# The prompt's memory projection laid into the turns of the dilated attention, with sixteen row buffers

## The chip, the cores and the metric

The kernel runs on one core of a Trainium2 chip. The metric is the device time of one execution in microseconds (us). The core has a matmul engine (TensorE, PE in the views, PEld for its weight loads), VectorE (DVE), ScalarE (ACT), GpSimd (POOL) and a sync engine (SP) that here only issues transfers. DMA transfers go over 16 DMA engines.

## The reference, cut to what matters

One layer of a decoder for a prompt of 1,024 rows and 32 sample rows. The change touches two of its parts, which don't depend on each other:

```python
def dilated_prompt(q, k, v, window, dil):      # for (128,1), (512,4), (2048,16), 4 heads of 64 each
    ...
    s = jnp.einsum('brnqhd,brnkhd->brnhqk', qs, kb).astype(jnp.float32) * ATTN_SCALE
    s = jnp.where(mask[None, None, :, None], s, -jnp.inf)
    lse = jax.nn.logsumexp(s, axis=-1)
    p = jnp.exp(s - lse[..., None])
    o = jnp.einsum('brnhqk,brnkhd->brnqhd', p.astype(vb.dtype), vb)
...
def mem_project(mem, w_mem_kv_l):              # mem is 256 x 1024, w_mem_kv_l is 1024 x 512
    return (mem @ w_mem_kv_l).reshape(mem.shape[0], mem.shape[1], 2, MEM_HEADS, HEAD_DIM)
```

The projection's result is an output of the step and feeds the memory attention much later.

## The kernel before, in words

`run_phases` calls the phases one after another. Each is a function with its own buffers and semaphores and a barrier of all engines at its end. In this order: `project_and_select`, `attend_window` (the dilated attention of the prompt), `mem_project` (the projection of the memory), `attend_sparse`, and then the sample rows, the merge, the memory attention and the feed-forward.

`attend_window` works through 24 jobs j, eight blocks of 128 queries in each of three groups (`B_JOBS`). A job whose block has a previous block in its window (`has_prev`: all but the first of group 0, every second of group 1, none of group 2) has 256 keys per head, the others 128. The work is a software pipeline over iterations `it`. In one iteration TensorE runs `turn(it+1)` (four transposes of queries and keys), `logits(it)`, `turn_probs(it-2)` (four or eight transposes of the probabilities) and `values(it-3)` (into columns 0 to 255 of the PSUM tile `p_o`, one bank of 512 columns). VectorE runs `soft(it)` (four masked copies with a minimum) and `take_probs(it-2)`. ScalarE runs `take_turned(it+1)`, `exp(it-1)`, `take_probs(it-2)` and `take_block(it-3)`, which empties `p_o` and issues the store of the job's result. Each engine runs its instructions in the written order. The rows of a job (queries, keys, values: 384 KB) come by SP's queue into one of `BR` = 7 buffers `b_row`; the load of job j >= 7 waits until `values(j-6)` is done. `soft(j)` waits until the store of job j-5 has landed (`OR` = 5 buffers `ob_row`). SP loads the memory (`m_in`, 1 MB) and its weight (`w_mem_raw`, 2 MB) behind the last rows.

`mem_project` then splits the weight into a high and a low part (`w_hi`, `w_lo`), transposes the memory by 16 transposes into PSUM, splits it too (`m_hi`, `m_lo`), multiplies by three products per block of 128 (48 matmuls of 512 columns), copies the results out (`k_row`, `vm`), transposes the keys and stores both.

Of the kernel before, what the change touches and what calls it, by code (L numbers as in the profile page):

```python
# [1109 lines left out]
BR, OR = 7, 5  # L1110
# [20 lines left out]
def attend_window(nc, d, m_in, w_raw):  # L1131

    ctx = ExitStack()
    with ctx:
# [11 lines left out]
        p_x = ps("p_x", [P, 512])  # L1146

        s_const = sem("w_const")
        s_brow = [sem(f"w_brow{u}") for u in range(BR)]
        s_mem = sem("w_mem")  # L1150
# [25 lines left out]
        with nc.Block() as block:  # L1176
            @block.sync
            def _(sp):
                sp.dma_start(ident[:, :], d["ident"]).then_inc(s_const, 16)
                sp.dma_start(masks[:, :], d["att_mask"]).then_inc(s_const, 16)  # L1180
                for j in range(NB_J):
                    g, u = B_JOBS[j]
                    if j >= BR:
                        sp.wait_ge(s_pv, j - BR + 2)
                    for p0, src in block_rows(d["z_b"][g], g, u):
                        sp.dma_start(b_row[p0:p0 + src.shape[0], j % BR, :], src).then_inc(s_brow[j % BR], 16)
                sp.dma_start(m_in[:, :, :], d["mem_prompt"].rearrange("(i p) c -> p i c", p=P)).then_inc(s_mem, 16)
                sp.dma_start(w_raw[:, :, :], d["w_mem_kv"][0].rearrange("(k p) c -> p k c", p=P)).then_inc(s_mem, 16)
                for j in range(NB_J - OR, NB_J):
                    sp.wait_ge(s_ob[j % OR], stored_b[j])  # L1190
                sp.wait_ge(s_mem, 32)
# [44 lines left out]
            def _(dve):  # L1236
# [27 lines left out]
                dve.wait_ge(s_const, 32)  # L1264
                for it in range(NB_J + 2):
                    if it < NB_J:
                        soft(it)
                    if 0 <= it - 2 < NB_J:
# [3 lines left out]
            def _(pe):  # L1272
# [33 lines left out]

                def values(j):
                    a, b = B_JOBS[j]
                    pe.wait_ge(s_ptA, j + 1)
                    if second[j]:  # L1310
                        pe.wait_ge(s_ptD, second[j])
                    if j:
                        pe.wait_ge(s_oev, j)
# [9 lines left out]
                pe.wait_ge(s_const, 32)  # L1323
# [729 lines left out]


def mem_project(nc, d, km_t, vm, m_in, w_raw):

    ctx = ExitStack()
    with ctx:
        sb, ps, sem = alloc(nc, ctx)
        ident = sb("ident5", [P, P])  # L2060
        m_hi = sb("m_hi", [P, KC, 2 * P], F32R)
        m_lo = sb("m_lo", [P, KC, 2 * P], F32R)
        w_hi = sb("w_hi5", [P, KC, 512], F32R)
        w_lo = sb("w_lo5", [P, KC, 512], F32R)
        k_row = sb("k_row5", [P, 2, 256])
        p_m = ps("p_m", [P, 4, 512])
        p_z = ps("p_z5", [P, 2, 512])
        p_k = ps("p_k5", [P, 512])
        s_in = sem("m_in_s")
        s_t = sem("m_t")  # L2070
        s_hi = sem("m_hi_s")
        s_lo = sem("m_lo_s")
        s_whi = sem("m_whi")
        s_wlo = sem("m_wlo")
        s_z = sem("m_z")
        s_ev = sem("m_ev")
        s_kt = sem("m_kt")
        s_ktev = sem("m_ktev")
        s_out = sem("m_out")
        with nc.Block() as block:  # L2080
            @block.sync
            def _(sp):
                sp.dma_start(ident[:, :], d["ident"]).then_inc(s_in, 16)
                for i in range(2):
                    sp.wait_ge(s_ev, 2 * i + 2)
                    sp.dma_start(d["new_mem_kv"][i * P:(i + 1) * P, 0:256], k_row[:, i, :]).then_inc(s_out, 16)
                    sp.dma_start(d["new_mem_kv"][i * P:(i + 1) * P, 256:512], vm[:, i, :]).then_inc(s_out, 16)
                sp.wait_ge(s_out, 64)

            @block.scalar  # L2090
            def _(act):
                for u in range(2):
                    act.activation(w_hi[:, 4 * u:4 * u + 4, :], w_raw[:, 4 * u:4 * u + 4, :], ACT.Copy).then_inc(s_whi, 1)
                act.wait_ge(s_t, 1)
                for q in range(4):
                    a = act.activation(m_hi[:, 2 * q:2 * q + 2, :].rearrange("p k c -> p (k c)"), p_m[:, q, :], ACT.Copy)
                a.then_inc(s_hi, 1)
                for i in range(2):
                    act.wait_ge(s_z, i + 1)
                    act.activation(k_row[:, i, :], p_z[:, i, 0:256], ACT.Copy).then_inc(s_ev, 1)  # L2100
                    act.activation(vm[:, i, :], p_z[:, i, 256:512], ACT.Copy).then_inc(s_ev, 1)
                act.wait_ge(s_kt, 1)
                act.activation(km_t[:, :, :].rearrange("p c k -> p (c k)"), p_k[:, :], ACT.Copy).then_inc(s_ktev, 1)

            @block.vector
            def _(dve):
                for u in range(2):
                    dve.wait_ge(s_whi, u + 1)
                    dve.tensor_tensor(w_lo[:, 4 * u:4 * u + 4, :], w_raw[:, 4 * u:4 * u + 4, :], w_hi[:, 4 * u:4 * u + 4, :].bitcast(F32), ALU.subtract).then_inc(s_wlo, 1)
                dve.wait_ge(s_hi, 1)  # L2110
                for q in range(4):
# [1486 lines left out]
```

## Time and profile before

| what | value |
|---|---|
| median of 3 runs | 2269.52 us (2265.06 to 2273.71) |
| profiled execution, its time | 2268.95 us |
| its span, first to last instruction | 2267.0 us |
| mean granted TensorE clock | 0.94 of full speed |
| `attend_window`, from its first transpose to its last store's issue | 747.1 to 860.8 us |
| `mem_project` with its barrier | 863.35 to 890.6 us |
| busy share of the span | PE 91%, DVE 57%, ACT 32%, POOL 26% |

Times in the views are microseconds from the span's start. The granted clock is given as a share of 2.4 GHz: 1.00 is 2.4 GHz, 0.50 is 1.2 GHz.

### The profile page before, as it was taken

The numbers are of one execution on the slowest core, as the hardware profiler recorded it, in microseconds if no ns is written. First come the engines' busy times: TensorE is split into PE (matmuls) and PEld (weight loads), VectorE is DVE, ScalarE is ACT, GpSimd is POOL, SyncE is SP. The second block draws the span as 40 slices with busy tenths as digits, with TensorE's granted clock in tenths as the row PEclk, the third lists the DMA queues.
The fourth block names the chain that finished last, engine by engine and source line by source line (L and its number), as shares of the span: only waits on it lengthen the run. The fifth ranks groups of instructions, "written<-read, shape, count | busy, mean of one in ns | idle before, by whom it ended". The sixth has DMA issues, their size and how long they took to land. (4 is left out here: it accounts for less than half of the span.)

```text
span 2267.0 us, 35384 instructions
## 1 busy us (share of the span) xinstructions
PE 2070.2 (91%) x13591; PEld 1897.8 (84%) x13591; DVE 1284.0 (57%) x2490; ACT 731.3 (32%) x1517; POOL 582.5 (26%) x680
## 2 busy tenths in 40 slices
PE   6899899999999885889779989969999999999995
PEld 5878788999999774555459989869999999999995
DVE  4049999998830322553327323677776677643644
ACT  5233222121120662334222224553233223332423
POOL 4786646768840001100200120110000000301000
PEclk9999999999996876799889998879999999999998
DMA  4122232347733443883326302012222222535333
GB/s 155 29 83 74 69 87 66 108 163 229 234 117 107 122 148 88 258 265 121 95 88 200 87 25 80 10 44 81 81 73 79 81 85 76 205 97 163 119 86 119
DMA packets 228891, 254.75 MB, mean 112 GB/s; under 512 B 52261, under 2 KB 211269, under 8 KB 228213
## 3 DMA queue, kind: packets, MB, share of 16 engines
q1 hardware_dynamic: 192820, 167.18, 25.0%
q0 software_dynamic: 9280, 55.45, 6.9%
q10 hardware_dynamic: 26624, 29.87, 3.7%
q8 instruction: 108, 1.77, 0.3%
q14 instruction: 59, 0.48, 0.1%
HBM read 205.77 MB, written 74.00 MB: 123 GB/s over the span
## 5 line engine op out<-in xcount | busy, mean ns | idle before, releaser
L935 PE MATMUL pz<-w_hi,n_hi 128*128 128x384 f32 (+2 forms) x720 | 246.6, 343 | 0.6 <-issue 0.3
L935 PE MATMUL pz<-w_hi,n_lo 128*128 128x384 f32 (+2 forms) x720 | 240.3, 334 | 0.0
L935 PE MATMUL pz<-w_lo,n_hi 128*128 128x384 f32 (+2 forms) x720 | 240.0, 333 | 0.0
L843 DVE MATCH_REPLACE8 sel<-m,sel 128x1024 f32<-128x1024 f32 (+4 forms) x224 | 205.2, 920 | 0.0
L840 DVE MAX8 m<-sel 128x8 f32<-128x1024 f32 (+4 forms) x224 | 197.5, 924 | 0.2
L3439 PE MATMUL p_c<-n_t_hi,blk 128*128 128x264 f32 x1152 | 196.6, 284 | 0.0
L3439 PEld LDWEIGHTS p_c<-n_t_hi,blk 128*128 128x128 f32 x1152 | 163.2, 188 | 0.0
L3439 PE MATMUL p_c<-mix_hi,blk 128*128 128x264 f32 x864 | 152.3, 289 | 10.5 <-DVE mix_lo L3251 6.7
L935 PEld LDWEIGHTS pz<-w_hi,n_hi 128*128 128x128 f32 x720 | 138.8, 193 | 22.9 <-issue 20.1
L935 PEld LDWEIGHTS pz<-w_lo,n_hi 128*128 128x128 f32 x720 | 138.7, 193 | 0.0
L935 PEld LDWEIGHTS pz<-w_hi,n_lo 128*128 128x128 f32 x720 | 138.7, 193 | 0.0
L3439 PEld LDWEIGHTS p_c<-mix_hi,blk 128*128 128x128 f32 x864 | 125.7, 193 | 10.8 <-issue 6.7
L941 PE MATMUL pz<-n_hi,w_hi 128*128 128x352 f32 x384 | 129.6, 338 | 4.8 <-ACT z L525 4.8
L941 PE MATMUL pz<-n_lo,w_hi 128*128 128x352 f32 x384 | 127.8, 333 | 0.0
L941 PE MATMUL pz<-n_hi,w_lo 128*128 128x352 f32 x384 | 127.7, 332 | 0.0
L531 ACT ACTIVATE z<-pz 128x384 f32<-128x384 f32 (+2 forms) x90 | 42.8, 475 | 249.8 <-PE pz L935 209.8
L693 POOL TENSOR_TENSOR w_lo<-w_raw,w_hi 128x1536 fp32r<-128x1536 f32 (+3 forms) x32 | 106.5, 3330 | 47.7 <-ACT w_hi L498 47.7
L3439 PE MATMUL p_c<-n_t_lo,blk 128*128 128x264 f32 x576 | 117.0, 284 | 0.0
L711 POOL TENSOR_TENSOR rot<-z,rope 128x384 f32<-128x384 f32 (+3 forms) x90 | 75.3, 836 | 153.7 <-ACT z L531 151.8
L1250 DVE CUSTOM_DVE_ANT_0 probs<-p_s,masks 128x128 f32<-128x128 f32 (+1 forms) x96 | 28.1, 349 | 152.4 <-PE p_s L1292 143.7
L3080 POOL DMA_DIRECT2D g_s<-gate x22 | 11.9, 543 | 388.8 <-DVE gate L3291 388.8
L3478 PE MATMUL p_c<-n_t_hi,blk 128*128 128x264 f32 x504 | 99.8, 287 | 2.4 <-DVE blk L3317 1.6
(466 smaller groups left out, 5322.3 us busy)
## 6 DMA issues: line engine op xcount, KB each, us to landing
w_raw<-in_w_in SPq DMA_DIRECT2D x26, 768.0 KB, 4.6
blk_raw<-in_w_ffn_in SPq DMA_DIRECT2D x74, 256.0 KB, 2.9
relu<-z_qb SPq DMA_DIRECT2D x24, 512.0 KB, 5.1
blk_raw<-in_w_ffn_out SPq DMA_DIRECT2D x58, 192.0 KB, 2.5
z_b<-z ACTq DMA_DIRECT2D x48, 192.0 KB, 1.9
gates<-z ACTq DMA_DIRECT2D x48, 176.0 KB, 2.7
gate<-gates SPq DMA_DIRECT2D x24, 352.0 KB, 3.6
out_new_win_sample<-in_cache_win_kv POOLq DMA_DIRECT2D x8, 1016.0 KB
```

The costliest lines, as they stand in the source:

```text
L531: act.activation(z[:, u, 0:w], pz[:, s % 2, 0:w], ACT.Copy).then_inc(s_zev, 1)
L693: pool.tensor_tensor(w_lo[:, n % 2, 4 * j:4 * j + 4, 0:w], w_raw[:, f % RAW, :, 0:w], w_hi[:, n % 2, 4 * j:4 * j + 4, 0:w].bitcast(F32), A ...
L711: pool.tensor_tensor(a, z[:, u, 0:nh * HD].rearrange("p (h e) -> p h e", h=nh), cos, ALU.mult)
L840: dve.max(out=m8[0:r, u, :], in_=sel[0:r, o:o + n]).then_inc(s_max, 1)
L843: dve.match_replace(out=sel[0:r, o:o + n], in_to_replace=m8[0:r, u, :], in_values=sel[0:r, o:o + n], imm_value=PICKED).then_inc(s_rep, 1)
L935: m = pe.matmul(out, tokens(a, k, i), b[:, n % 2, k, 0:w], start=(k == 0 and p == 0), stop=(k == KC - 1 and p == 2))
L941: m = pe.matmul(out, a[:, n % 2, k, i * P:(i + 1) * P], b[:, k, third * THIRD:(third + 1) * THIRD], start=(k == 0 and p == 0), stop=(k == ...
L1250: t = dve.tensor_tensor_reduce(out=probs[:, u, h * w:(h + 1) * w], in0=p_s[:, j % 2, c:c + w], in1=masks[:, m0:m0 + w], scale=-ATT_SCALE, ...
L3080: pool.dma_start(d["g_s"][f * P:(f + 1) * P, half * HALF:(half + 1) * HALF], (gate, u3)[half][:, :, :].rearrange("p a c -> p (a c)")).then ...
L3439: m = pe.matmul(p_c[:, 2 * x + q, 0:QUART], a[:, w], b[:, q * QUART:(q + 1) * QUART], start=(k == 0 and y == 0), stop=(k == 3 and y == 2))
L3478: last = pe.matmul(p_c[:, x % 6, 0:QUART], a[:, cols], b[:, q * QUART:(q + 1) * QUART], start=(f == 0 and y == 0), stop=(f == FC - 1 and y ...
```

## The change

`mem_project` is gone as a phase. Its work is spread over the iterations of `attend_window` by the table `SIDE`, whose keys are jobs. Ahead of `values(j)` TensorE runs `side(j)`: for jobs 3 to 10 two transposes of the memory ("m"), for jobs 13, 14, 18 and 20 a chain of 24 matmuls of 256 columns ("z"), for jobs 16 and 17 two transposes of the keys ("t"). All write to `p_side`, the columns 256 to 511 of the same bank as `p_o`. VectorE empties it by `take_side(j)`, placed behind `soft(j+4)`, and the next `side` or `values` on TensorE waits for that. VectorE also splits the weight, one eighth in each of the iterations 8 to 15. The row buffers `b_row` go from 7 to 16. SP loads the masks behind the first rows, the memory ahead of job 6's rows and the weight ahead of job 9's. The projection's two halves are stored by SP behind all row loads.

```diff
@@ -1107,7 +1107,7 @@
 
 B_JOBS = [(g, u) for g in range(3) for u in range(NT)]
 NB_J = len(B_JOBS)
-BR, OR = 7, 5
+BR, OR = 16, 5
 PAGED = 6
 OBW = 264
 
@@ -1128,7 +1128,14 @@
     return [(0, v[2 * u, :, :]), (64, v[2 * u + 1, :, :])]
 
 
-def attend_window(nc, d, m_in, w_raw):
+SIDE = {3 + k: ("m", k, 0) for k in range(KC)}
+SIDE.update({13: ("z", 0, 0), 14: ("z", 1, 0), 16: ("t", 0, 0), 17: ("t", 1, 0), 18: ("z", 0, 1), 20: ("z", 1, 1)})
+SIDE_NO = {j: n + 1 for n, j in enumerate(sorted(SIDE))}
+SIDE_OF = {SIDE[j]: SIDE_NO[j] for j in SIDE}
+SPLIT_FROM = 8
+
+
+def attend_window(nc, d, km_t, vm):
 
     ctx = ExitStack()
     with ctx:
@@ -1144,10 +1151,25 @@
         p_t = ps("p_t", [P, 2, 512])
         p_o = ps("p_o", [P, 512])
         p_x = ps("p_x", [P, 512])
-
-        s_const = sem("w_const")
+        p_side = p_o[:, 256:512]
+        m_in = sb("m_in", [P, 2, D])
+        m_hi = sb("m_hi", [P, KC, 2 * P], F32R)
+        m_lo = sb("m_lo", [P, KC, 2 * P], F32R)
+        w_raw = sb("w_mem_raw", [P, KC, 512])
+        w_hi = sb("w_hi5", [P, KC, 512], F32R)
+        w_lo = sb("w_lo5", [P, KC, 512], F32R)
+        k_row = sb("k_row5", [P, 2, 256])
+
+        s_ident = sem("w_ident")
+        s_mask = sem("w_mask")
+        s_min = sem("w_min")
+        s_wraw = sem("w_wraw")
+        s_whi = sem("w_whi")
+        s_wlo = sem("w_wlo")
+        s_mhi = sem("w_mhi")
+        s_side = sem("w_side")
+        s_new = sem("w_new")
         s_brow = [sem(f"w_brow{u}") for u in range(BR)]
-        s_mem = sem("w_mem")
         s_xt = sem("w_xt")
         s_xev = sem("w_xev")
         s_qk = sem("w_qk")
@@ -1176,19 +1198,26 @@
         with nc.Block() as block:
             @block.sync
             def _(sp):
-                sp.dma_start(ident[:, :], d["ident"]).then_inc(s_const, 16)
-                sp.dma_start(masks[:, :], d["att_mask"]).then_inc(s_const, 16)
+                sp.dma_start(ident[:, :], d["ident"]).then_inc(s_ident, 16)
                 for j in range(NB_J):
                     g, u = B_JOBS[j]
+                    if j == 1:
+                        sp.dma_start(masks[:, :], d["att_mask"]).then_inc(s_mask, 16)
+                    if j == 6:
+                        sp.dma_start(m_in[:, :, :], d["mem_prompt"].rearrange("(i p) c -> p i c", p=P)).then_inc(s_min, 16)
+                    if j == 9:
+                        sp.dma_start(w_raw[:, :, :], d["w_mem_kv"][0].rearrange("(k p) c -> p k c", p=P)).then_inc(s_wraw, 16)
                     if j >= BR:
                         sp.wait_ge(s_pv, j - BR + 2)
                     for p0, src in block_rows(d["z_b"][g], g, u):
                         sp.dma_start(b_row[p0:p0 + src.shape[0], j % BR, :], src).then_inc(s_brow[j % BR], 16)
-                sp.dma_start(m_in[:, :, :], d["mem_prompt"].rearrange("(i p) c -> p i c", p=P)).then_inc(s_mem, 16)
-                sp.dma_start(w_raw[:, :, :], d["w_mem_kv"][0].rearrange("(k p) c -> p k c", p=P)).then_inc(s_mem, 16)
+                for half, kept in enumerate((k_row, vm)):
+                    for i in range(2):
+                        sp.wait_ge(s_side, SIDE_OF[("z", i, half)])
+                        sp.dma_start(d["new_mem_kv"][i * P:(i + 1) * P, 256 * half:256 * half + 256], kept[:, i, :]).then_inc(s_new, 16)
                 for j in range(NB_J - OR, NB_J):
                     sp.wait_ge(s_ob[j % OR], stored_b[j])
-                sp.wait_ge(s_mem, 32)
+                sp.wait_ge(s_new, 64)
 
             @block.scalar
             def _(act):
@@ -1261,10 +1290,33 @@
                         dve.wait_ge(s_pv, j - 1)
                     dve.tensor_copy(probs_t[:, j % 2, 512:w], p_t[:, 1, 0:w - 512]).then_inc(s_ptD, 1)
 
-                dve.wait_ge(s_const, 32)
+                def split_weight(k):
+                    dve.wait_ge(s_wraw, 16)
+                    dve.tensor_copy(w_hi[:, k, :], w_raw[:, k, :]).then_inc(s_whi, 1)
+                    dve.wait_ge(s_whi, k + 1)
+                    dve.tensor_tensor(w_lo[:, k, :], w_raw[:, k, :], w_hi[:, k, :].bitcast(F32), ALU.subtract).then_inc(s_wlo, 1)
+
+                def take_side(j):
+
+                    kind, a, b = SIDE[j]
+                    dve.wait_ge(s_oev, j + 1)
+                    if kind == "m":
+                        dve.tensor_copy(m_hi[:, a, :], p_side).then_inc(s_mhi, 1)
+                        dve.wait_ge(s_mhi, a + 1)
+                        dve.tensor_tensor(m_lo[:, a, :], p_side, m_hi[:, a, :].bitcast(F32), ALU.subtract).then_inc(s_side, 1)
+                    elif kind == "z":
+                        dve.tensor_copy((vm if b else k_row)[:, a, :], p_side).then_inc(s_side, 1)
+                    else:
+                        dve.tensor_copy(km_t[:, a, :], p_side).then_inc(s_side, 1)
+
+                dve.wait_ge(s_mask, 16)
                 for it in range(NB_J + 2):
                     if it < NB_J:
                         soft(it)
+                    if it - 4 in SIDE:
+                        take_side(it - 4)
+                    if 0 <= it - SPLIT_FROM < KC:
+                        split_weight(it - SPLIT_FROM)
                     if 0 <= it - 2 < NB_J:
                         take_probs(it - 2)
 
@@ -1304,13 +1356,35 @@
                         m = pe.transpose(p_t[:, c // 4, c % 4 * P:(c % 4 + 1) * P], probs[:, j % 3, c * P:(c + 1) * P], ident[:, :])
                     m.then_inc(s_pt, 1)
 
+                def side(j):
+
+                    kind, a, b = SIDE[j]
+                    if SIDE_NO[j] > 1:
+                        pe.wait_ge(s_side, SIDE_NO[j] - 1)
+                    if kind == "m":
+                        pe.wait_ge(s_min, 16)
+                        for i in range(2):
+                            pe.transpose(p_o[:, 256 + i * P:256 + (i + 1) * P], m_in[:, i, a * P:(a + 1) * P], ident[:, :])
+                    elif kind == "z":
+                        pe.wait_ge(s_wlo, KC)
+                        for k in range(KC):
+                            for p, (x, y) in enumerate(((m_hi, w_hi), (m_lo, w_hi), (m_hi, w_lo))):
+                                pe.matmul(p_side, x[:, k, a * P:(a + 1) * P], y[:, k, 256 * b:256 * b + 256], start=(k == 0 and p == 0), stop=(k == KC - 1 and p == 2))
+                    else:
+                        for i in range(2):
+                            pe.transpose(p_o[:, 256 + i * P:256 + (i + 1) * P], k_row[:, i, a * P:(a + 1) * P], ident[:, :])
+
                 def values(j):
                     a, b = B_JOBS[j]
+                    if j:
+                        pe.wait_ge(s_oev, j)
+                    if j in SIDE:
+                        side(j)
+                    elif j - 1 in SIDE:
+                        pe.wait_ge(s_side, SIDE_NO[j - 1])
                     pe.wait_ge(s_ptA, j + 1)
                     if second[j]:
                         pe.wait_ge(s_ptD, second[j])
-                    if j:
-                        pe.wait_ge(s_oev, j)
                     slots = ([(j - 1) % BR] if has_prev(a, b) else []) + [j % BR]
                     c = 0
                     for h in range(BH):
@@ -1320,7 +1394,7 @@
                             c += 1
                     m.then_inc(s_pv, 1)
 
-                pe.wait_ge(s_const, 32)
+                pe.wait_ge(s_ident, 16)
                 for it in range(LAST):
                     for j in turns[it]:
                         turn(j)
@@ -2050,88 +2124,6 @@
                 for c in range(4):
                     t = pe.transpose(p_n[:, c * NS:(c + 1) * NS], o_row[:, c * P:(c + 1) * P], ident[0:NS, 0:NS])
                 t.then_inc(s_ot, 1)
-
-
-def mem_project(nc, d, km_t, vm, m_in, w_raw):
...
-            @block.tensor
-            def _(pe):
-                pe.wait_ge(s_in, 16)
-                for k in range(KC):
-                    for i in range(2):
-                        t = pe.transpose(p_m[:, k // 2, (k % 2 * 2 + i) * P:(k % 2 * 2 + i + 1) * P], m_in[:, i, k * P:(k + 1) * P], ident[:, :])
-                t.then_inc(s_t, 1)
-                pe.wait_ge(s_lo, 1)
-                pe.wait_ge(s_wlo, 2)
-                for i in range(2):
-                    for k in range(KC):
-                        for p, (a, b) in enumerate(((m_hi, w_hi), (m_lo, w_hi), (m_hi, w_lo))):
-                            m = pe.matmul(p_z[:, i, :], a[:, k, i * P:(i + 1) * P], b[:, k, :], start=(k == 0 and p == 0), stop=(k == KC - 1 and p == 2))
-                    m.then_inc(s_z, 1)
-                pe.wait_ge(s_ev, 4)
-                for c in range(2):
-                    for i in range(2):
-                        t = pe.transpose(p_k[:, (2 * c + i) * P:(2 * c + i + 1) * P], k_row[:, i, c * P:(c + 1) * P], ident[:, :])
-                t.then_inc(s_kt, 1)
 
 
 class InverseRoot:
@@ -3502,11 +3494,7 @@
                 inv_ffn = on(outer, "inv_ffn", [P, T])
                 km_t = inv_ffn[:, 0:4 * P].rearrange("p (c k) -> p c k", c=2)
                 vm = inv_ffn[:, 4 * P:8 * P].rearrange("p (c k) -> p c k", c=2)
-                with ExitStack() as loaded:
-                    m_in = on(loaded, "m_in", [P, 2, D])
-                    w_raw = on(loaded, "w_mem_raw", [P, KC, 512])
-                    attend_window(nc, d, m_in, w_raw)
-                    mem_project(nc, d, km_t, vm, m_in, w_raw)
+                attend_window(nc, d, km_t, vm)
                 oa = [on(mixers, f"oa_{x}", [P, 4, T], F32R) for x in ("hi", "lo")]
                 kv_pages = on(choice, "kv_pages", [P, PAGED, NPG, 2 * P], side="right")
                 early = {x: on(choice, f"{x}_early", shape, side="right") for x, shape in
```

Three places show how the instructions move. The first is TensorE's order around iteration 8, where `p_x` is the tile of `turn`, `p_s` that of `logits`, `p_t` that of `turn_probs`. Before:

```order
L1278 MATMUL p_x<-ident,b_row 128x128 x4
L1292 MATMUL p_s<-qk_t 128x128 x4
L1304 MATMUL p_t<-ident,probs 128x128 x8
L1318 MATMUL p_o<-b_row,probs_t 128x64 x8
L1278 MATMUL p_x<-ident,b_row 128x128 x4
```

And after:

```order
L1330 MATMUL p_x<-ident,b_row 128x128 x4
L1344 MATMUL p_s<-qk_t 128x128 x4
L1356 MATMUL p_t<-ident,probs 128x128 x8
L1367 MATMUL p_o<-ident,m_in 128x128 x2
L1392 MATMUL p_o<-b_row,probs_t 128x64 x8
L1330 MATMUL p_x<-ident,b_row 128x128 x4
```

Two transposes of the memory now stand between `turn_probs` and `values`. The second is VectorE's order at the same place, the end of `soft(8)` and what follows it. Before:

```order
L1250 ISA probs,ob_row<-p_s,masks 128x128
L1250 ISA ob_row 128x1
L1262 COPY probs_t<-p_t 128x512
L1250 ISA probs,ob_row<-p_s,masks 128x256
L1250 ISA ob_row 128x1
```

And after:

```order
L1279 ISA probs,ob_row<-p_s,masks 128x128
L1279 ISA ob_row 128x1
L1304 CAST m_hi<-p_o 128x256
L1306 TENSOR_TENSOR m_lo<-p_o,m_hi 128x256
L1295 CAST w_hi<-w_mem_raw 128x512
L1297 TENSOR_TENSOR w_lo<-w_mem_raw,w_hi 128x512
L1291 COPY probs_t<-p_t 128x512
```

The first two of the four new instructions are `take_side(4)`, for which TensorE's next `side` waits; the other two are one eighth of the weight's split. The third place is TensorE's order at iterations 16 and 17, after the change (24 matmuls in each chain, of which the last three of the first and the first of the second are shown):

```order
L1372 MATMUL p_o<-w_hi,m_hi 128x256
L1372 MATMUL p_o<-w_hi,m_lo 128x256
L1372 MATMUL p_o<-w_lo,m_hi 128x256
L1392 MATMUL p_o<-b_row,probs_t 128x64 x8
L1330 MATMUL p_x<-ident,b_row 128x128 x4
L1344 MATMUL p_s<-qk_t 128x128 x4
L1356 MATMUL p_t<-ident,probs 128x128 x8
L1372 MATMUL p_o<-w_hi,m_hi 128x256
```

A chain of the projection now stands ahead of `values` in each of them.

## Rows read from the trace of the kernel before

**Rows 1.** The page's first part: the span.

```profile
span 2267.0 us, 35384 instructions
```

**Rows 2.** Waits between 743 and 862 us: us in total, times, longest.

```profile
PE p_x L1278 <- DMA b_row<-z_b: 12.8, 8, 7.0
...
DVE probs L1250 <- DMA o_b<-ob_row: 8.8, 3, 4.5
```

**Rows 3.** Windows: length, busy per engine, then clock, DMA share, GB/s.

```profile
757.00:806.00 49.00, 47.44 (x463) 43.46 (x461) 22.20 (x113) 41.01 (x139) 0.00 (x0) 1.00 0.44 112
807.00:816.00 9.00, 8.91 (x49) 7.83 (x50) 2.26 (x10) 4.38 (x15) 0.00 (x0) 0.50 0.23 69
817.00:823.00 6.00, 4.67 (x45) 4.27 (x43) 1.62 (x9) 4.03 (x15) 0.00 (x0) 1.00 0.36 98
824.00:840.00 16.00, 16.00 (x86) 14.32 (x84) 2.80 (x24) 8.83 (x34) 0.00 (x0) 0.50 0.30 88
841.00:850.00 9.00, 5.79 (x54) 5.03 (x52) 1.95 (x19) 6.49 (x28) 0.00 (x0) 1.00 0.98 343
```

**Rows 4.** Timeline, iteration 6 at full clock: start, us, engine, line.

```profile
770.05 1.26 PE L1292 MATMUL p_s<-qk_t 64*128 64x128 f32 x16
771.25 1.09 PE L1304 MATMUL p_t<-ident,probs 128*128 128x128 f32 x8
772.18 1.90 PE L1318 MATMUL p_o<-b_row,probs_t 128*128 128x64 f32 x16
772.74 0.69 DVE L1262 COPY probs_t<-p_t 128x512 f32<-128x512 f32 x1
773.91 0.61 PE L1278 MATMUL p_x<-ident,b_row 128*128 128x128 f32 x4
```

**Rows 5.** Timeline of TensorE, iterations 15 and 18 at half clock.

```profile
807.09 1.08 PE L1278 MATMUL p_x<-ident,b_row 128*128 128x128 f32 x4 [1.84 <-DMA b_row<-z_b]
808.11 2.24 PE L1292 MATMUL p_s<-qk_t 64*128 64x128 f32 x16
810.28 1.97 PE L1304 MATMUL p_t<-ident,probs 128*128 128x128 f32 x8
812.03 1.81 PE L1318 MATMUL p_o<-b_row,probs_t 128*128 128x64 f32 x8
...
822.98 0.63 PE L1278 MATMUL p_x<-ident,b_row 128*128 128x128 f32 x4 [1.33 <-DMA b_row<-z_b]
...
825.46 3.51 PE L1318 MATMUL p_o<-b_row,probs_t 128*128 128x64 f32 x16
828.76 1.06 PE L1278 MATMUL p_x<-ident,b_row 128*128 128x128 f32 x4
```

**Rows 6.** VectorE by form: line, operation, tiles, count, busy, mean ns.

```profile
L1262 DVE COPY probs_t<-p_t 128x512 f32<-128x512 f32 x11 | 7.6, 687 | 0.6 <-PE p_t L1304 0.4
L2703 DVE TENSOR_TENSOR om_lo<-p_x,om_hi 128x256 fp32r<-128x256 f32 x8 | 3.4, 420 | 1.6 <-ACT om_hi L2584 1.6
```

**Rows 7.** Timeline of ScalarE at the end of the phase.

```profile
846.68 0.37 ACT L1219 ACTIVATE ob_row<-p_o 128x256 f32<-128x256 f32 x1
...
850.26 0.36 ACT L1219 ACTIVATE ob_row<-p_o 128x256 f32<-128x256 f32 x1
```

**Rows 8.** The stores of one line, L1223.

```profile
DMA to landing us min/median/max: 1.8/3.3/6.3
```

**Rows 9.** Timeline at the phases' borders.

```profile
859.67 1.10 ACTq L1223 DMA_DIRECT2D o_b<-ob_row  x2
863.35 0.34 SPq L2083 DMA_DIRECT2D ident<-in_ident  x1
...
890.60 0.34 SPq L1467 DMA_DIRECT2D cur_a<-in_att_mask  x1
```

**Rows 10.** Timeline of TensorE in the feed-forward, matmuls of 264 columns.

```profile
1701.35 0.64 PE L3439 MATMUL p_c<-mix_hi,blk 128*128 128x264 f32 x4
1701.84 0.40 PE L3439 MATMUL p_c<-mix_lo,blk 128*128 128x264 f32 x2
```

More of the change, by code:

```diff
@@ L2052, in _ @@
                 t.then_inc(s_ot, 1)
-def mem_project(nc, d, km_t, vm, m_in, w_raw):
[L2057 to L2083, printed above, removed]
-                for i in range(2):
[L2085 to L2097, printed above, removed]
-                for i in range(2):
[L2099 to L2111, printed above, removed]
-                    a = dve.tensor_tensor(m_lo[:, 2 * q:2 * q + 2, :].rearrange("p k c -> p (k c)"), p_m[:, q, :],
-                                          m_hi[:, 2 * q:2 * q + 2, :].rearrange("p k c -> p (k c)").bitcast(F32), ALU.subtract)
-                a.then_inc(s_lo, 1)
-            @block.tensor
-            def _(pe):
-                pe.wait_ge(s_in, 16)
-                for k in range(KC):
-                    for i in range(2):
-                        t = pe.transpose(p_m[:, k // 2, (k % 2 * 2 + i) * P:(k % 2 * 2 + i + 1) * P], m_in[:, i, k * P:(k + 1) * P], ident[:, :])
-                t.then_inc(s_t, 1)
-                pe.wait_ge(s_lo, 1)
-                pe.wait_ge(s_wlo, 2)
-                for i in range(2):
-                    for k in range(KC):
-                        for p, (a, b) in enumerate(((m_hi, w_hi), (m_lo, w_hi), (m_hi, w_lo))):
-                            m = pe.matmul(p_z[:, i, :], a[:, k, i * P:(i + 1) * P], b[:, k, :], start=(k == 0 and p == 0), stop=(k == KC - 1 and p == 2))
-                    m.then_inc(s_z, 1)
-                pe.wait_ge(s_ev, 4)
-                for c in range(2):
-                    for i in range(2):
-                        t = pe.transpose(p_k[:, (2 * c + i) * P:(2 * c + i + 1) * P], k_row[:, i, c * P:(c + 1) * P], ident[:, :])
-                t.then_inc(s_kt, 1)
```

## The prediction

> **What bounds the kernel now.** I read the page's span first [rows 1], then the waits of the dilated attention [rows 2] and the granted clock over its length [rows 3], because the change lies in this phase and the one behind it, and both run one after the other with every other phase: what they lose or gain is the whole effect. The profiled execution took 2268.95 us, 1.95 more than its span and 0.57 under the median of the runs, so the sum is made against 2268.95 and 0.6 is added at the end.
>
> TensorE is what the phase runs at while its clock is full: from 757 to 806 it is busy 47.4 of 49 us at 1.00 [rows 3]. One iteration with previous blocks takes 1.20 for logits, 0.93 for turn_probs and 1.73 for values, read as distances between starts from 770.05 to 773.91 [rows 4], and 0.53 for turn (its row says 0.61, of which some overlaps), 4.39 in all. VectorE has room: its soft begins when logits ends at 771.31 and its copy behind soft begins at 772.74 [rows 4]. At half clock the same pieces take 1.02, 2.17, 1.75 and, for values without previous blocks 1.6 (1.81 as a row), with them 3.3 [rows 5], so 8.2 for a full iteration.
>
> The clock is the second thing. TensorE stood 1.84 us waiting for rows before 807.09 and 1.33 before 822.98 [rows 5]; behind each the clock is 0.50, over 807 to 816 and 824 to 840, though TensorE is busy nearly all of that [rows 3]. All waits for rows together are 12.8 us, of which 7.0 is the start of the phase, so 5.8 inside it [rows 2]. From 841 to 850, with 3.2 of 9 us idle in several pieces, the clock held [rows 3]; the largest of them lies behind the stores' waits (8.8 us in three) [rows 2]. So a single stop above about 1.3 us is what costs clock here, and the half-speed stretches behind the two cover the windows of 9 and 16 us.
>
> The projection is a plain addition: from 863.35 to 890.60, 27.25 us with its barrier [rows 9].
>
> **Removed.** The whole 27.25 [rows 9]: nothing of it stays in its place, since the attention's last store is issued at 859.67 as before and the next phase starts where the projection's first transfer was issued. Sixteen buffers let the 24 row loads run far ahead, so the 5.8 us of row waits should go. The masks' move behind the first rows is under one issue, counted as nothing.
>
> **Added on TensorE.** 16 transposes for the memory and 4 for the keys: a turn has four in 0.53, so 0.27 for two at full clock and 0.5 at half. Four chains of 24 matmuls: 264 columns come every 0.12 (0.49 for four) at full clock [rows 10], so 2.9 a chain; at half clock double the columns' time, 24 x 0.22 = 5.3.
>
> **Added wait.** This decides. values(j) in iteration j+3 now waits for take_side(j-1), which VectorE runs in the same iteration behind soft(j+3), and soft waits for logits(j+3), which ends just ahead of turn_probs on TensorE. In the rows of iteration 6: VectorE reaches the copy behind soft at 772.74 while values starts at 772.18 [rows 4]. take_side for "m" is a cast and a subtraction of 256 columns, the second 0.42 by its row; the first lies under the 0.69 of 512 columns, taken as 0.42 too [rows 6]. With 0.1 each for the wait of one on the other and for TensorE's wait (bounds 0 and 0.2) values could start at 772.74 + 0.42 + 0.42 + 0.2 = 773.8, 1.6 later than now. Queued behind it is everything on TensorE: values, the next turn, the next logits; VectorE and ScalarE then wait for these, so nothing else fills the hole. It happens in iterations 7 to 14 (eight times) and, with one copy instead of two and with half-sized soft, at about 1.1 in iterations 17, 18, 20, 21, 22 and 24. Turns without previous blocks have a shorter soft and a shorter turn_probs, which about cancel, so 1.6 stands for all eight. At half clock turn_probs takes 0.8 more while VectorE doesn't change, so 0.8 for a full iteration and about 1.2 where turn_probs has four transposes.
>
> The weight's split adds about 1.3 us to VectorE in iterations 8 to 15. It is hidden: soft 1.43, take_side 0.94, split 1.3 and copy 0.69 are 4.4 in iterations that now last 6 us or more; without that cover it would cost nothing up to 4.4.
>
> **Which clock.** A hole of 1.6 is between the 1.33 and 1.84 that were each followed by half clock [rows 5], and it comes once in every iteration. At half clock the hole shrinks to 0.8 to 1.2, and recovery took 9 and 16 us or more of nearly uninterrupted work before [rows 3]. So I expect about a quarter of the time at full clock in iterations 7 to 14, and full clock around the chains, which are dense.
>
> Iterations 7 to 14 took 773.91 to 807.09 [rows 4, 5], 33.2. All at full clock: less 2.6 of row waits (1.84, and 0.8 of the 2.6 that are left of 5.8 after 1.84 and 1.33), plus 8 x 1.6 = 12.8, plus 8 x 0.27 = 2.2: 45.6. All at half: eight turns 8.0, logits four at 2.17 and four at 1.1, turn_probs five at 1.75 and three at 0.9, values six at 3.3 and two at 1.6, together 56; holes 7.4; transposes 4; that is 67. With a quarter of the time at full clock a third of the work runs there, 0.33 x 45.6 + 0.67 x 67 = 60: plus 27.
>
> Iterations 15 to 18 took 807.09 to 828.76, 21.7, mostly at half clock [rows 3, 5]. Now: 6.5 at half; 3.0 + 2.1 + 1.6 + 1.7 = 8.4 with the first chain, in which the clock rises; at full clock 3.0 + 0.5 + 2.9 = 6.4 and 3.5 + 1.2 = 4.7. Sum 26: plus 4. All at full clock it is 3.5 + 3.5 + 3.2 + 3.5 = 13.7 (the pieces of iteration 6, halved where there is no previous block), 5.8 of chains and 1.9 of waits, 21.4; all at half 6.5 + 11.6 + 11.1 + 7.0 = 36.
>
> From iteration 19 to the end, 828.76 to 863.35: ScalarE empties a block every 3.58 [rows 7], plus 0.5 where it also takes a turn, so about 4.1 against 4.6 of TensorE at half clock (1.0 + 1.1 + 0.9 + 1.6) and 2.6 at full. Two chains and four waits fall here, part of them into ScalarE's surplus: plus 6 (1.5 if the clock is full, 12 if it is half).
>
> Stores: with ten megabytes queued at once the stores land late; they took up to 6.3 us while 3 MB was queued, 3.3 usually [rows 8]. soft(j) needs the store issued three iterations before, some 5 to 6 us earlier at full clock: plus 1, bounds 0 and 5.
>
> Sum: 27 + 4 + 6 + 1 - 27.25 = plus 10.8, so 2279.7 profiled and 2280 as a median.
>
> **A rule against this.** The rows say that stops of 1.33 and 1.84 us were followed by half clock [rows 5]. The Trainium skill (TensorE: Matmul & The Clock Gate, Why this matters for your kernels) warns only of idle stretches longer than any of these between bursts of matmuls. By that rule the clock would hold through the change's holes, and the sum would be 2256 instead of 2280; that is the first rival below. The trace disagrees with it so far.
>
> **The rivals.** First, the clock holds: the holes stay at 1.6 but the work between them runs at full speed. For it: the clock held from 841 to 850 with 36% idle [rows 3]. Then 45.6 - 33.2 = 12.4, 21.4 - 21.7 = -0.3, and 1.5, less 27.25: minus 13.6, 2256. This is faster, and it decides from about 60% of the time at full clock. Chance 0.15. Second, the clock stays at half almost throughout: 34 + 14 + 12 - 27.25 = plus 33, 2302. For it: TensorE never works 10 us without a hole in iterations 7 to 14. Against: the chains are dense. Chance 0.17. Third, VectorE's copies are done under other work and the hole is not there: 2.2 - 2.6 = -0.4, then 13.7 + 5.8 - 21.7 = -2.2, less 27.25: 2240. The program order speaks against it. Chance 0.05. Fourth, the stores land so late in the first fifteen iterations that soft waits each time: 5 on top of the forecast, about 2286 to 2292; the 8.8 us of such waits at the end of the phase speak for it [rows 2], the longer iterations against. Chance 0.08. My forecast, mixed clock, has 0.55, by itself 2266 to 2294.
>
> **How the numbers follow.** Half a per cent is 11.3 us, about what a measurement of this kernel can tell: faster is below 2258, slower above 2281. The forecast lies at that border, so I split its 0.55 into 0.33 within and 0.22 above. Faster: 0.13 of the first rival and the third, 0.18. Slower: 0.22, 0.17 and 0.06, 0.45. Same: 0.37. The range leaves out the third rival and the upper end of the second: 2252 to 2298.
>
> **What would show it.** TensorE waiting for VectorE's side copy at `values` and `side` 14 times, 0.8 to 1.7 us each; no waits for rows but the first; clock well under 1 from the seventh iteration to the first chain; the next phase starting about 10 us later than now. Wrong if the waits are under 1 us at full clock, or if the clock in iterations 7 to 14 is above 0.8.

## The result and the profile after

The changed kernel takes 2248.43 us (median, 2244.56 to 2251.37) against 2271.61 us measured beside it, a ratio of 0.9901 (95% interval 0.9872 to 0.9931). Measured again beside its variants it gave 0.9932 (0.9907 to 0.9957). It is faster by 15 to 23 us; the forecast was 2280 and slower.

The prediction said that TensorE would stop in front of `side` and `values`. It does. The timeline of the changed kernel in iteration 7 (start, length, engine, line):

```profile
772.68 1.26 PE L1344 MATMUL p_s<-qk_t 64*128 64x128 f32 x16
773.87 1.09 PE L1356 MATMUL p_t<-ident,probs 128*128 128x128 f32 x8
...
775.36 0.42 DVE L1304 CAST m_hi<-p_o 128x256 fp32r<-128x256 f32 x1
775.82 0.42 DVE L1306 TENSOR_TENSOR m_lo<-p_o,m_hi 128x256 fp32r<-128x256 f32 x1
...
776.34 0.41 PE L1367 MATMUL p_o<-ident,m_in 128*128 128x128 f32 x2 [1.38 <-issue]
776.59 1.90 PE L1392 MATMUL p_o<-b_row,probs_t 128*128 128x64 f32 x16
```

VectorE empties the side tile from 775.36 to 776.24 behind its soft, and TensorE, done with turn_probs at 774.96, starts again at 776.34. Against the start that rows 4 would give (0.93 behind the start of turn_probs, 774.80) this is 1.54 late; 1.6 was predicted. As idle time it is 1.38.

What did not come is the half clock. The windows of the changed kernel over iterations 7 to 14, cut at the clock's changes (length, busy time per engine, then clock, DMA share, GB/s), answer to [rows 3]:

```profile
772.14:778.00 5.86, 4.48 (x46) 3.99 (x45) 3.54 (x14) 3.42 (x11) 0.00 (x0) 1.00 0.38 106
779.00:781.00 2.00, 2.00 (x13) 1.65 (x13) 0.60 (x5) 1.64 (x6) 0.00 (x0) 0.50 0.51 126
782.00:795.00 13.00, 10.26 (x96) 9.14 (x95) 8.33 (x29) 7.01 (x23) 0.00 (x0) 1.00 0.28 83
796.00:798.00 2.00, 2.00 (x16) 1.67 (x16) 0.00 (x0) 1.54 (x7) 0.00 (x0) 0.50 0.48 99
799.00:817.00 18.00, 12.85 (x117) 11.06 (x116) 12.83 (x50) 10.43 (x34) 0.00 (x0) 1.00 0.15 45
```

The clock fell twice, behind holes, and was back within 4 us each time. From 799 to 817 it held although TensorE was idle for 5 of 18 us in four holes. The stages, in the same columns (iterations 7 to 14, 15 to 18, 19 to the next phase):

```profile
772.14:817.60 45.46, 36.19 (x309) 31.53 (x308) 26.58 (x102) 26.32 (x88) 0.00 (x0) 0.92 0.27 78
817.60:838.71 21.11, 19.52 (x178) 17.91 (x178) 7.08 (x38) 12.40 (x44) 0.00 (x0) 1.00 0.12 40
838.71:873.87 35.16, 25.58 (x202) 22.73 (x201) 6.10 (x44) 18.17 (x68) 0.00 (x1) 0.86 0.16 43
```

Before, they took 33.2, 21.7 and 34.6 us [rows 4, 5, 9]. So +12.3, -0.6 and +0.6; the stretch from the first transpose to iteration 7 grew by 0.5, and the 27.25 us of the projection are gone: -14.5, from 143.5 to 129.0 us between the first transpose and the start of the next phase. The other 4.4 us of the profiles' difference in span lie outside that stretch, 2.2 ahead of the first transpose (0.8 of it in the wait for the first rows) and 2.2 behind; the first transpose alone stands anywhere from 737.7 to 749.7 in the fourteen profiles taken here, so I don't read a cause into them.

The waits between 743 and 875 us (us in total, times, longest), beside [rows 2]:

```profile
PE p_x L1330 <- DMA b_row<-z_b: 7.3, 2, 6.2
DVE probs L1279 <- DMA o_b<-ob_row: 6.1, 2, 4.0
```

Only 1.1 us of row waits is left beside the first, and it too lies at the start (747 us), where the kernel before had 0.86. The waits for stores didn't grow in sum, but they moved: of the 8.8 us before, 7.1 lay at the end of the phase; the 6.1 now lie in iterations 5 and 6, where `soft` begins 1.4 to 1.7 us late. TensorE didn't stop for it, since it needs these probabilities two iterations later.

### The profile page after: what moved, and what is told of

It reads as the page before. It is cut to its first block and busy times, and to the rows that moved or that the text cites. A ratio compares the mean times of both kernels' runs of the same rounds, so it can differ in the third digit from the quotient of the medians.

```text
span 2248.1 us, 35492 instructions
## 1 busy us (share of the span) xinstructions
PE 2055.4 (91%) x13639; PEld 1884.3 (84%) x13639; DVE 1295.6 (58%) x2522; ACT 723.5 (32%) x1506; POOL 582.3 (26%) x680
## 5 line engine op out<-in xcount | busy, mean ns | idle before, releaser
L3431 PE MATMUL p_c<-mix_hi,blk 128*128 128x264 f32 x864 | 151.9, 289 | 10.8 <-DVE mix_lo L3243 6.7
```

Of the source, the lines that this page charges most:

```text
L3431: m = pe.matmul(p_c[:, 2 * x + q, 0:QUART], a[:, w], b[:, q * QUART:(q + 1) * QUART], start=(k == 0 and y == 0), stop=(k == 3 and y == 2))
```

## The experiments

All ratios are to the kernel before, measured on the same chip beside the variant. Since other phases vary by several microseconds between executions, the profiles are compared by the stretch of iterations 7 to 14 alone. The theories: **length** (a hole costs only its length) against **clock** (it also brings half clock, as the prediction had it).

**The buffers alone.** The kernel before with one number changed:

```diff
-BR, OR = 7, 5
+BR, OR = 16, 5
```

> The kernel before with 16 row buffers and nothing else of the change; the projection stays a phase of its own. Theory A (the waits for rows cost their length and, by the half clock behind them, as much again): the 5.8 us of row waits inside the dilated attention go and with them the 9 us and 16 us stretches at half clock; the phase gets 10 to 12 us shorter, about 2260 against 2271.6. Theory B (only the waits' own length is at stake, the half clock has another cause): 5 us or less, 2266 or more.

Measured: 0.9969 (0.9951 to 0.9986), 7 us less. Iterations 7 to 14, with clock and DMA columns as above:

```profile
776.16:806.02 29.86, 29.86 (x295) 27.55 (x294) 11.76 (x61) 24.53 (x85) 0.00 (x0) 1.00 0.59 179
```

TensorE never stops and the clock is full: 29.9 us instead of 33.2. The phase with the projection took 133.3 us instead of 143.5, 10.2 less, as theory A has it. The total's interval, 3 to 11 us, leaves both theories open, so that the row waits cost more than the 5.8 us they last rests on one profile of each kernel. In this one a 2 us stop at 811 us, for VectorE, which had itself waited for a store, still cost clock.

**The change with seven buffers.**

```diff
-BR, OR = 16, 5
+BR, OR = 7, 5
```

> The changed kernel with 7 row buffers instead of 16. Theory A (the buffers are what keeps the clock up): row waits of 1 to 2 us come back on top of the holes, the clock falls behind them, 8 to 12 us more than the changed kernel, 2257 to 2260. Theory B (the side work stretches the iterations enough that seven buffers would do): 2249, within 2 us of the changed kernel.

Measured: 0.9983 (0.9962 to 1.0005), 12 to 19 us above the changed kernel by its two measurements. Most of what the change gains is gone. Iterations 7 to 14 took 53.2 us at a mean clock of 0.78, with only 4.7 us of row waits in the phase behind its start:

```profile
770.86:824.02 53.16, 43.18 (x308) 37.60 (x308) 25.86 (x99) 26.44 (x88) 0.00 (x0) 0.78 0.39 113
```

**The hole taken away.** VectorE empties the side tile ahead of its soft:

```diff
                 for it in range(NB_J + 2):
+                    if it - 4 in SIDE:
+                        take_side(it - 4)
                     if it < NB_J:
                         soft(it)
-                    if it - 4 in SIDE:
-                        take_side(it - 4)
```

> The changed kernel with VectorE emptying the side tile ahead of its soft instead of behind it, so that TensorE's wait for it should be over before turn_probs ends. Theory A (a hole costs its own length, the clock holds): the 12.9 us of holes in front of side and values in iterations 7 to 22 go, less what ScalarE's pace takes back in the last group: 9 to 13 us less than the changed kernel, 2236 to 2240. Theory B (the pace is set by ScalarE or by the stores, the holes only show it): 3 us or less. Theory C (soft is now late by 0.9 us and that is a new wait): no gain or a loss.

Measured: 0.987 (0.9839 to 0.9902) in 4 runs, so it was measured again with the same code:

> The order with the side tile emptied ahead of soft once more (0.987 in its first 4 runs, of wide interval). It has no holes in iterations 7 to 14. Theory A (a hole costs its own length only): 10 to 13 us below the changed kernel, 0.9845 to 0.9855 if that stands at 0.990. Theory B (holes also cost clock): 15 us or more below the changed kernel measured beside it.

Measured: 0.9862 (0.9839 to 0.9885), 2235.05 us, beside 0.9932 for the changed kernel: 16 us less, with an interval of some 8 to 24, in which theory A's 10 to 13 also lie. The profiles tell more: iterations 7 to 14 alone are 13 and 16 us shorter than in the changed kernel's two profiles, where the holes' length gives 10.8 (worked out in the next part). Iteration 7 of the first of the two:

```profile
772.49 1.26 PE L1344 MATMUL p_s<-qk_t 64*128 64x128 f32 x16
772.57 0.42 DVE L1304 CAST m_hi<-p_o 128x256 fp32r<-128x256 f32 x1
773.03 0.42 DVE L1306 TENSOR_TENSOR m_lo<-p_o,m_hi 128x256 fp32r<-128x256 f32 x1
773.68 1.09 PE L1356 MATMUL p_t<-ident,probs 128*128 128x128 f32 x8
773.79 0.42 DVE L1279 CUSTOM_DVE_ANT_0 probs<-p_s,masks 128x256 f32<-128x256 f32 x1 [0.34 <-PE p_s L1344]
...
774.61 0.38 PE L1367 MATMUL p_o<-ident,m_in 128*128 128x128 f32 x2
```

The two copies now lie under the logits, in time in which VectorE waited for them anyway; soft starts as early as before, and side follows turn_probs without a stop. Both profiles have 32.4 us in iterations 7 to 14 at full clock, that is the 29.9 of the buffers alone and 2.5 for the side transposes (2.2 predicted, for eight pairs; seven fall here). The first of the two:

```profile
771.95:804.40 32.45, 31.92 (x308) 29.11 (x308) 26.58 (x100) 25.85 (x88) 0.00 (x0) 1.00 0.37 108
```

**The hole made longer.** The split of the weight ahead of the side tile's emptying:

```diff
+                    if 0 <= it - SPLIT_FROM < KC:
+                        split_weight(it - SPLIT_FROM)
                     if it - 4 in SIDE:
                         take_side(it - 4)
-                    if 0 <= it - SPLIT_FROM < KC:
-                        split_weight(it - SPLIT_FROM)
```

> The changed kernel with one eighth of the weight's split (0.42 and 0.69 us on VectorE) placed ahead of the emptying of the side tile in iterations 8 to 15: seven holes (iterations 8 to 14) longer by 1.1 us, 2.4 instead of 1.3. Theory A (a hole costs its own length): 7 x 1.1, about 8 us more than the changed kernel, 2256, clock near 1.00 between the holes. Theory B (holes above some size bring half clock, as the prediction had it from 1.3 on): half clock through most of iterations 8 to 14, 20 us and more on top, 2275 to 2280.

Measured: 1.0027 (1.0008 to 1.0047), 21 to 29 us above the changed kernel by its two measurements, where 8 us of wait was added. Iterations 7 to 14:

```profile
775.34:842.21 66.87, 51.24 (x309) 45.12 (x308) 26.06 (x100) 26.44 (x88) 0.00 (x0) 0.66 0.18 54
```

This is what the prediction had described for the change itself: two thirds of the stretch at half clock.

Two sizes between, with additions whose result nothing reads, ahead of `take_side` in iterations 7 to 14 (n is 1 or 2):

```diff
+                    for x in range(n if 7 <= it <= 14 else 0):
+                        dve.tensor_tensor(hole[:, 256 * x:256 * x + 256], masks[:, 0:256], masks[:, 128:384], ALU.add)
                     if it - 4 in SIDE:
                         take_side(it - 4)
```

> The changed kernel with one addition of 256 columns (0.35 us between starts, its result unused) ahead of the emptying of the side tile in iterations 7 to 14: holes of about 1.7 us instead of 1.4. Theory A (cost rises with the length alone until well over 2 us): 8 x 0.35, 3 us more than the changed kernel, 0.9915 of before. Theory B (the clock gives way gradually between 1.4 and 2.4 us): 6 to 12 us more, 0.993 to 0.9955. Theory C (there is an edge just above 1.4 us): 20 us more, 0.999.

> The same with two such additions: holes of about 2.1 us. Theory A (length alone): 8 x 0.7, 6 us more than the changed kernel, 0.9925 of before. Theory B (gradual loss of clock): 12 to 20 us more, 0.9955 to 0.999. Theory C (edge): 24 us more, 1.0005; the run with 2.4 us holes in seven iterations stood at 1.0027.

Measured: 0.9973 (0.995 to 0.9996) and 1.0024 (1.0001 to 1.0047), 9 and 21 us above the changed kernel at 0.9932. Iterations 7 to 14 of the two:

```profile
774.24:827.95 53.71, 42.19 (x308) 37.41 (x308) 29.15 (x108) 26.43 (x88) 0.00 (x0) 0.81 0.23 65
771.39:834.21 62.82, 48.45 (x308) 42.48 (x308) 32.41 (x120) 26.45 (x88) 0.00 (x0) 0.71 0.20 58
```

And one size below: soft's last head behind the emptying of the side tile, so that the hole is one head shorter:

```diff
                     for h in range(BH):
+                        if h == BH - 1 and 7 <= j <= 14:
+                            take_side(j - 4)
...
-                    if it - 4 in SIDE:
+                    if it - 4 in SIDE and not 7 <= it <= 14:
                         take_side(it - 4)
```

> The changed kernel with the side tile emptied ahead of the last of soft's four heads in iterations 7 to 14: holes shorter by one head, 1.0 instead of 1.4 us with previous blocks, 1.1 instead of 1.3 without. Theory A (length alone): about 2.4 us less than the changed kernel measured beside it. Theory B (clock is lost gradually from about 1 us on): 5 to 10 us less.

Measured: 0.9928 (0.9905 to 0.9951), 1 us less than the changed kernel, inside the interval: the total can't tell the two theories apart here. Its profile has 41.0 us in iterations 7 to 14 at clock 1.00. But half a microsecond past the end of that stretch, behind the eighth hole (1.08 us), the clock fell for some 3 us:

```profile
778.10:819.07 40.97, 32.96 (x309) 28.99 (x308) 25.86 (x99) 26.08 (x88) 0.00 (x0) 1.00 0.30 85
...
817.26 1.97 PE L1394 MATMUL p_o<-b_row,probs_t 128*128 128x64 f32 x16 [1.08 <-issue]
...
820.00:821.00 1.00, 1.00 (x11) 1.00 (x11) 0.00 (x0) 0.89 (x4) 0.00 (x0) 0.50 0.38 135
```

So holes of about 1 us are not free of the risk either; in this execution one of eight was followed by half clock. This stretch is 4.5 and 7.8 us shorter than the changed kernel's two, and yet the runs differ by 1 us, so whether other executions kept the clock as well as this one isn't shown.

**The changed kernel again.**

> The changed kernel once more, in more rounds and beside its variants, with a second profile. Theory A (its holes of 1.4 us cost clock in some executions and not in others): the ratio lies above the first measurement's 0.9901, up to 0.994, and iterations 7 to 14 (45.5 us in the first profile) take longer, 48 to 52. Theory B (below an edge the clock is safe): 0.990 again and 45 to 46 us.

Measured: 0.9932 and 48.8 us. In this profile the clock fell behind the first hole and stayed at half for nearly 14 us while TensorE did not stop, then held through four holes of 1.29 to 1.38 us, and fell behind the fifth for nearly 7 us:

```profile
772.37:778.00 5.63, 4.25 (x44) 3.76 (x43) 3.48 (x14) 3.42 (x11) 0.00 (x0) 1.00 0.36 97
779.00:791.00 12.00, 12.00 (x64) 10.54 (x64) 4.29 (x18) 6.06 (x21) 0.00 (x0) 0.50 0.31 88
792.00:817.00 25.00, 19.27 (x178) 16.81 (x178) 15.51 (x59) 14.45 (x48) 0.00 (x0) 1.00 0.25 74
820.00:825.00 5.00, 5.00 (x30) 4.45 (x30) 0.55 (x3) 2.51 (x10) 0.00 (x0) 0.50 0.08 27
```

The same code so spends a different share at half clock from one execution to the next. Its 12 run times reach from 2241.2 to 2262.3; the nine of the order without holes from 2233.5 to 2239.1.

**The holes without the work.** The buffers alone, plus two unread additions behind soft in iterations 7 to 14, for which `values` waits (the projection is where it was):

```diff
+                    if 7 <= it <= 14:
+                        for x in range(2):
+                            t = dve.tensor_tensor(hole[:, 256 * x:256 * x + 256], masks[:, 0:256], masks[:, 128:384], ALU.add)
+                        t.then_inc(s_hole, 1)
...
+                    if 4 <= j <= 11:
+                        pe.wait_ge(s_hole, j - 3)
```

> The kernel before with 16 row buffers, the projection still a phase of its own, and only the holes of the change: in iterations 7 to 14 VectorE runs two additions of 256 columns into a tile that nothing reads behind soft (0.42 us each), and values waits for them. So TensorE waits as in the changed kernel without having its side work. Theory A (a hole of 1.3 us costs little beyond its length): eight of them, 10 to 12 us over the run with 16 buffers alone (0.9969 of before), so 1.0015 to 1.0025 of before. Theory B (such holes bring half clock for most of the stretch): 20 us and more over it, 1.006 or more.

Measured: 1.0007 (0.9987 to 1.0027), about 9 us over the buffers alone, with an interval from some 3 to 14. That speaks for length alone, or a little clock. The profiled execution was the slowest of 13, 10 us above their median, and has 49.2 us in iterations 7 to 14 at 0.77:

```profile
772.11:821.28 49.17, 41.57 (x294) 36.32 (x294) 18.07 (x85) 26.43 (x88) 0.00 (x0) 0.77 0.43 135
```

That is 19.3 us more than with the buffers alone, 7.6 of it idle time and 11.7 the same work at the lower clock. So the holes bring half clock without the side work too, in some executions much and at the median little.

**Seven buffers without holes.** The order of the hole's removal with `BR` = 7:

> The changed kernel with the side tile emptied ahead of soft (no holes) and with 7 row buffers. Theory A (row waits cost the clock by themselves, as in the kernel before): about 7 us over the same order with 16 buffers, which stood at 0.987, so 0.990. Theory B (row waits and holes add up to the 18 us that 7 buffers cost with the holes in place, and neither alone costs much clock): 3 us or less, 0.988.

Measured: 0.9895 (0.9863 to 0.9928), 6 to 8 us above the same with 16 buffers (0.987 and 0.9862), with intervals that overlap. Its profile agrees: 37.9 us in iterations 7 to 14, 5.5 more than with 16 buffers, for 3.5 us of row waits, of which one lasted 2.61 and was followed by some 3 us at half clock.

```profile
765.51:803.41 37.90, 34.01 (x309) 31.01 (x308) 26.24 (x99) 26.35 (x89) 0.00 (x0) 0.95 0.55 158
```

With the holes in place the same seven buffers cost 12 to 19 us. That the two cost more together than apart is likely but not clear of noise.

**Stores on SP.** The last eight blocks' stores issued by SP, in turn with the projection's stores, instead of by ScalarE, on top of the order without holes (cut to the line on ScalarE):

```diff
...
-                    for p0, dst in block_rows(d["o_b"][g], g, u):
+                    for p0, dst in block_rows(d["o_b"][g], g, u) if j < 16 else []:
...
```

> The side tile emptied ahead of soft, and the stores of the last eight blocks issued by SP instead of ScalarE, where each pair holds ScalarE for 1.1 us ahead of its exponentials. Theory A (ScalarE paces the last group, 3.6 us a block against 2.6 on TensorE): 4 to 8 us less than the same without it. Theory B (the stores' landing and VectorE's wait for it pace it, or SP's issues come late behind its waits): 2 us or less, or more time.

Measured: 0.985 (0.9827 to 0.9873), 2234.11 us, beside 0.9862: 3 us less, inside the intervals. The profiles show it where the edit lies: from iteration 19 to the next phase 30.7 us (826.29 to 857.03) against 33.6 (827.14 to 860.78), and the same 51.8 us in iterations 7 to 18 of both. So ScalarE's issues cost some 3 us at the end, less than the 4 to 8 of theory A. The order without holes beats both kernels, by 29 to 34 us against before, with or without this.

## Why the prediction was wrong, point by point

**The removal** (27.25 us) and **the side work** were right: 32.4 us without holes at full clock against 30.6 + 2.2 predicted. **The row waits** inside the phase went, about 5 of the 5.8 us; the other 0.9 was the wait for the second rows at the phase's start, which stayed (1.1 us, and 2.4 in the second profile).

**The added wait** was right in place and order: 1.54 against 1.6 us in iteration 7. Eight times 1.6, 12.8, was 2 too much: by their length the eight come to 10.8 (below). Iteration 8 has a half-sized `soft` beside a whole `turn_probs`, which the prediction took to cancel; there the hole is shorter, 0.65 us beside 1.03 with one head less, and at half clock it is gone. Behind the chains the holes were 0.4 to 0.9 us instead of 1.1.

**"Which clock" failed.** The step said that a hole of 1.6 us, since it lies between the idle times 1.33 and 1.84 behind which the clock had fallen [rows 5], brings half clock once in an iteration, that recovery takes 9 and 16 us, and so that a quarter of the time is at full clock. By the mean clocks of 0.92 and 0.84 it was 84% and 68%. Two stops were taken as a rule for all, and the two stretches at half clock of one trace as what a recovery costs. In the change's two profiles twelve stops of 1.29 to 1.38 us came at full clock, and four of them were followed by half clock. These four stretches lasted under 4 us twice, nearly 14 and nearly 7. The prediction also set a delay of starts (1.6) beside idle times (1.33, 1.84); the idle time of the same hole is 1.38, still between the two but at the lower edge. And it held that TensorE never works 10 us without a hole; in the second profile it did for 15 us (776.57 to 791.89), since at half clock the hole of iteration 8 was gone.

The stretch took 45.5 and 48.8 us; the forecast was 60. The sum for full clock was 45.6, and that it met the first profile is luck: its holes were 2 too long, and the 2.3 us (5.6 in the second) of lower clock are not in it. The terms behind it followed: iterations 15 to 18 took 21.1 (22.9 in the second profile) where full clock gave 21.4 and the forecast 26, and the end grew by 0.6 instead of 6. The stores cost TensorE nothing instead of 1. (`soft(j)` needs the store that ScalarE issues two iterations before, not three.)

The first rival, in which the clock holds through every hole, gave minus 13.6 us, 2256. The phase lost 14.5 us in the first profile and 8.5 in the second, so this was far nearer, by the two errors above that nearly cancel. As a rule it does not hold here either: the clock fell behind stops of 1.38 and 1.29 us in the changed kernel (at 779 and 796) and of 1.33 and 1.84 before [rows 5]. The reason that the prediction gave for it was misread as well: the clock held from 841 to 850, but that window ends inside the largest stop, and behind it the clock fell:

```profile
850.45 0.63 PE L1304 MATMUL p_t<-ident,probs 128*128 128x128 f32 x4 [2.11 <-ACT probs L1205]
...
854.03 1.08 PE L1304 MATMUL p_t<-ident,probs 128*128 128x128 f32 x4 [1.44 <-ACT probs L1205]
```

The Trainium skill (TensorE: Matmul & The Clock Gate, Why this matters for your kernels) warns only of idle stretches longer than all of these between bursts of matmuls. The traces disagree with it: stops of 1.29 to 2.11 us were followed by half clock.

How the clock's part grows with the hole can be read from the profiles. Without holes the stretch is 32.4 (29.9 without side work). The holes of one head less cost 8.6, at full clock throughout, so by length those of the change cost 8.6 and eight heads (four of 0.35 and four of 0.21, 2.2), 10.8. What is over is the clock:

| kernel | hole at full clock, idle us | 7 to 14, us | by length | over it | mean clock | 15 to 18, us |
|---|---|---|---|---|---|---|
| side tile first | 0 | 32.4, 32.4 | 32.4 | 0 | 1.00 | 19.4, 19.4 |
| one head shorter | 1.0 | 41.0 | 41.0 | 0 | 1.00 | 22.2 |
| the change | 1.4 | 45.5, 48.8 | 43.2 | 2.3, 5.6 | 0.92, 0.84 | 21.1, 22.9 |
| one addition | 1.7 | 53.7 | 46.0 | 7.7 | 0.81 | 22.6 |
| two additions | 2.1 | 62.8 | 48.8 | 14 | 0.71 | 22.7 |
| split first | 2.4 | 66.9 | 51.0 | 16 | 0.66 | 23.3 |

"By length" is what the stretch would take if the clock stayed full; it adds 8 x 0.35 for each addition and 7 x 1.11 for the split. The mean clock is that of iterations 7 to 14. The last column shows what that stretch cuts off: with the chains' own waits, iterations 15 to 18 take 21.1 us at full clock, and 1 to 2 more where a fall behind the last holes reaches into them. Each row but two rests on one profiled execution, and executions differ by a few microseconds; the order and the run times (0.9862, 0.9928, 0.9932, 0.9973, 1.0024, 1.0027) agree. So the mechanism, holes cost clock, was right, and it was sized for holes of 2.1 to 2.4 us.

The table doesn't say that the length of a single stop decides. In these kernels a longer hole is also more idle time in all, and no run separates the two. Two places speak against the single stop alone. The one of 2.61 us with seven buffers and no holes brought only some 3 us at half clock. And in the run of the buffers alone the clock fell at 835 us behind four stops of 0.6 to 0.8 us each:

```profile
828.72 0.66 PE L1278 MATMUL p_x<-ident,b_row 128*128 128x128 f32 x4 [0.64 <-ACT qk_t L1199]
830.78 0.63 PE L1304 MATMUL p_t<-ident,probs 128*128 128x128 f32 x4 [0.76 <-ACT probs L1205]
832.83 0.66 PE L1278 MATMUL p_x<-ident,b_row 128*128 128x128 f32 x4 [0.59 <-ACT qk_t L1199]
834.89 0.86 PE L1304 MATMUL p_t<-ident,probs 128*128 128x128 f32 x4 [0.76 <-ACT probs L1205]
...
836.00:837.00 1.00, 1.00 (x7) 1.00 (x6) 0.00 (x0) 0.71 (x2) 0.00 (x0) 0.50 0.39 95
```

What decides in a single execution whether a hole of 1.4 us is followed by half clock, and for how long, stays open; no run here settles it.

## What to carry to other kernels

When work is laid into another loop's gaps, ask in what order the emptying engine takes it: a copy that stands behind the work that depends on the matmuls just issued stops the matmul engine for its whole length, and ahead of it the same copy can be free; here that was worth nearly as much again as the change. Short stops should be judged by idle time in the same measure as the rows they are compared with, and the price of a fallen clock by many stops, not by the two worst of one trace. Cut a window behind the last stop and what follows it, not inside it. Here the kernel whose stops brought half clock in some executions and not in others also scattered more from run to run (21 us beside 6).

## What was not expected

Eight holes of about 1.0 us in successive iterations left the clock at 1.00 until the last of them, and holes of 2.1 us cost 14 us on top of their own 16. Seven buffers cost 12 to 19 us with the holes in place; without them it was 6 to 8, not clear of noise.
